# Half of the gate chunk's late adaptive units moved from TensorE to VectorE

## The reference, cut to what matters

```python
mod_l = jnp.split((silu(c) @ w_ada + b_ada)[:, None, :], 6, axis=-1)   # 2048 x 12288
mod_c = jnp.split((silu(c_ctx) @ w_ada + b_ada)[None, None, :], 6, axis=-1)
n_lat = modulate(rmsnorm(x, g_norm1), mod_l[0], mod_l[1])
n_ctx = modulate(rmsnorm(ctx, g_norm1), mod_c[0], mod_c[1])
...
z_lat = n_lat @ w_in ; z_ctx = n_ctx @ w_in[:, :o_g]     # columns U (S5), V (recurrence), gates
ya = s5_mixer(U) ; yb = lru_mixer(V) * gelu(z_lat[..., o_g:o_ga])
m = sigmoid(z_lat[..., o_ga:o_gb]) * (ya @ w_proj_a) + sigmoid(z_lat[..., o_gb:]) * (yb @ w_proj_b)
h_lat = x + mod_l[2] * (m @ w_out)
f_lat = modulate(rmsnorm(h_lat, g_norm2), mod_l[3], mod_l[4])
h_lat = h_lat + mod_l[5] * peer_ffn(f_lat, ...)
```

## Time and profile before

| | |
|---|---|
| time, median of 3 runs | 2298.59 us (2296.38 to 2298.80) |
| profiled execution: its time, its span | 2300.83 us, 2299.0 us |
| mean granted TensorE clock in it | 0.985 of full speed |
| busy: PE, DVE, ACT, POOL | 2000.0, 1369.5, 472.4, 1056.5 us |
| HBM read, written | 772.12 MB, 9.47 MB |

### The profile page before, as it was taken

How to read it: one execution, slowest core, us unless ns; L and a number is a source line. 1 busy time by engine, 2 the same in 40 slices (tenths; PEclk the granted TensorE clock), 3 DMA queues, 4 the chain that set the end, 5 groups by cost and what they waited for, 6 DMA issues and landing times.

```text
span 2299.0 us, 21921 instructions
## 1 busy us (share of the span) xinstructions
PE 2000.0 (87%) x8122; PEld 1158.5 (50%) x8122; DVE 1369.5 (60%) x2153; ACT 472.4 (21%) x1019; POOL 1056.5 (46%) x929
## 2 busy tenths in 40 slices
PE   6999999999999999979997998978877777777776
PEld 3443348888888878755553544423322222222222
DVE  5645964788873434774565455556556665655644
ACT  3116740344431000111101110111111011111011
POOL 0012323898991100164554445655555555555542
PEclk9999999999999999989999999999999999999999
DMA  9977885445558998899999999999999999999996
GB/s 338 336 226 201 313 302 173 135 144 147 147 150 301 355 325 297 314 392 415 422 421 413 421 420 419 422 421 421 422 421 422 421 421 421 421 422 422 421 422 271
DMA packets 249598, 787.26 MB, mean 342 GB/s; under 512 B 25578, under 2 KB 162994, under 8 KB 174354
## 3 DMA queue, kind: packets, MB, share of 16 engines
q0 software_dynamic: 83792, 574.96, 61.4%
q1 hardware_dynamic: 154020, 201.45, 26.4%
q10 hardware_dynamic: 11680, 9.44, 1.3%
HBM read 772.12 MB, written 9.47 MB: 340 GB/s over the span
## 4 chain that ended last, share of the span: by engine, by line
PE 45%; DMA 36%; POOL 13%; issue 4%; DVE 2%; ACT 1%; ACTq 0%; DVEq 0%; POOLq 0%
DMA vb<-in_peer_v,eidx 33%; PE ps L2396 14%; PE ps L1355 8%; PE ps L2255 5%; PE ps L2317 4%; PE ps L1562 4%; PE ps L1325 3%; PE ps L1340 2%; POOL vb L1767 1%; PE ps L1591 1%; PE ps L1300 1%; POOL nT L1767 1%; POOL big L609 1%; POOL big L578 1%; POOL big L581 1%
## 5 line engine op out<-in xcount | busy, mean ns | idle before, releaser
L2396 PE MATMUL ps<-vb,diag 128*128 128x512 f32 x2048 | 943.9, 609 | 229.8 <-DMA vb<-in_peer_v,eidx 227.7
L2396 PEld LDWEIGHTS ps<-vb,diag 128*128 128x128 f32 x2048 | 378.2, 192 | 782.5 <-issue 403.7
L1767 POOL DMA_INDIRECT vb<-in_peer_v,eidx x256 | 403.2, 1575 | 516.8 <-PE ps L2396 498.3
L2176 DVE CUSTOM_DVE_ANT_0 nT<-nT,f 128x2048 f32<-128x2048 f32 x167 | 381.9, 2291 | 315.0 <-DMA nT<-in_peer_u,eidx 314.6
L1355 PE MATMUL ps<-nT,w_ring 128*128 128x256 f32 (+1 forms) x1472 | 381.6, 417 | 0.0
L1355 PEld LDWEIGHTS ps<-nT,w_ring 128*128 128x128 f32 x1472 | 276.2, 190 | 95.6 <-issue 65.9
L2176 DVE CUSTOM_DVE_ANT_0 mT<-mT,f 128x2048 f32<-128x2048 f32 x84 | 192.2, 2292 | 158.3 <-DMA mT<-in_peer_u,eidx 158.0
L1767 POOL DMA_INDIRECT nT<-in_peer_u,eidx x167 | 190.6, 1141 | 68.4 <-issue 49.7
L1940 ACT ACTIVATE gel<-hd 128x2 f32<-128x2 f32 (+1 forms) x130 | 26.2, 202 | 905.8 <-DVE hd L2176 905.7
L2317 PE MATMUL ps<-fT,w_ring 128*128 128x256 f32 x448 | 101.2, 385 | 8.5 <-issue 7.8
L1767 POOL DMA_INDIRECT mT<-in_peer_u,eidx x84 | 93.4, 1112 | 32.1 <-issue 25.0
(11 more groups left out here) (416 smaller groups left out, 2176.5 us busy)
## 6 DMA issues: line engine op xcount, KB each, us to landing
w_ring<-in_w_ada SPq DMA_DIRECT2D x80, 1024.0 KB, 8.4
w_ring<-in_w_in SPq DMA_DIRECT2D x50, 1024.0 KB, 8.1
w_ring<-in_w_ada POOLq DMA_DIRECT2D x16, 1024.0 KB, 5.7
w_ring<-in_peer_w_query SPq DMA_DIRECT2D x16, 1024.0 KB, 17.6
w_ring<-in_w_proj_b SPq DMA_DIRECT2D x8, 1024.0 KB, 7.1
w_ring<-in_w_proj_a SPq DMA_DIRECT2D x8, 1024.0 KB, 7.4
w_ring<-in_w_out SPq DMA_DIRECT2D x8, 1024.0 KB, 6.3
vb<-in_w_out SPq DMA_DIRECT2D x5, 1024.0 KB, 12.8
```

What stands on the lines that cost most here:

```text
L1767: pool.indirect_dma_start(row, None, table, bass.IndirectOffsetOnAxis(ap=eidx[:, i % 3, j:j + 1], axis=0))\
L2176: v.tensor_tensor_reduce(u_buffer(m), u_buffer(m), f[:, i // HEADS], 1.0, 0.0, ALU.mult, ALU.add, hd[:, i % 2, m % K:m % K + 1]).then_inc( ...
L2396: last = pe.matmul(ps[:, 4 * tile + c, :], diag[:, m % NDIAG], vb[m % NV][:, c * 512:(c + 1) * 512], start=(r == 0), stop=(r == HEADS * K ...
```

## The change

Units 0 to 7 of chunk 2 become rows. There are now 24 rows: 0 to 7 of chunk 2, 8 to 23 of chunk 3, all through slot 4. Rows 0 to 3 are used ahead of the recurrence (`EARLY_ROWS`), 4 to 18 in it, two in each step and one in the last, 19 to 23 behind the multiplies of gate columns 0, 1, 4, 5 and 6 (`GATE_ROWS`). TensorE keeps units 8 to 15 of chunk 2, one in each column from U column 8 on. The sum of rows 0 to 7 has its own place (`first_sums`, two pieces of 1024 columns, one of them the memory of `kzero`), and `last_rows(0)` adds it into bank 6 behind gate column 5. `late_rows(0)` moves from the end of the recurrence to the place behind gate column 6. GpSimd loads rows 1 to 4 ahead of the first U store, rows 21 to 23 behind the loads of L562, and only then does `store_mods(0)`. Slot 4 returns to the ring when row 23 is used, and the gate columns' halves stay in slots 0 to 2.

```diff
-LATE_PER_PAIR = {3: (1, 0), 4: (3, 1), 5: (3, 1), 6: (3, 1), 7: (2, 1)}
+LATE_PER_PAIR = {3: (1, 0), 4: (1, 1), 5: (1, 1), 6: (1, 1), 7: (1, 0)}
+ON_VECTOR, EARLY_ROWS, GATE_ROWS = 8, 4, (0, 1, 4, 5, 6)
...
-        late = [(c, k) for c in LATE_CHUNKS for k in range(KD)]
+        late = [(LATE_CHUNKS[0], k) for k in range(ON_VECTOR, KD)]
+        rows = [(LATE_CHUNKS[0], k) for k in range(ON_VECTOR)] + [(c, k) for c in LATE_CHUNKS[1:] for k in range(KD)]
+        n_rows = ON_VECTOR + KD
...
-        freed_by[4] = (last_used, KD)
+        freed_by[4] = (last_used, n_rows)
...
-        last_wide = n + 1
-        n_slot = [turn[(2 * last_wide + 2) % 3]]
+        first_stage = len(pairs) - NSTAGE
+        for n in range(n + 2, first_stage):
+            plan_first(n, turn[2 * n % 3])
+            plan_second(n, turn[(2 * n + 1) % 3])
+        n_slot = [turn[2 * first_stage % 3]]
...
-        for n in range(last_wide + 1, len(pairs)):
+        for n in range(first_stage, len(pairs)):
             plan_first(n, next_slot())
             plan_second(n, next_slot())
...
-        kzero = sb("kzero", [H, G, H])
+        kz_all = sb("kzero", [P, G * H])
+        kzero = kz_all[0:H].rearrange("p (g h) -> p g h", g=G)
+        first_b = sb("first_b", [P, D - G * H])
         Cc = sb("Cc", [P, 2, G, H])
...
+        first_sums = [(kz_all, 0, G * H), (first_b, G * H, D)]
...
+        rows_of = [0, ON_VECTOR] + [ON_VECTOR + q * KD for q in range(1, NLATE)]
...
                     pool.wait_ge(last_used, k)
-                at = LATE_CHUNKS[1] * D
+                c, k = rows[k]
+                at = c * D
                 pool.dma_start(row_view(w_ring[:, 4]), t["w_ada"][0, k * P:(k + 1) * P, at:at + D])\
...
+            for n in range(1, EARLY_ROWS + 1):
+                load_row(n)
             for k in range(KW):
-                if 2 * k + 2 < KD:
-                    load_row(2 * k + 2)
+                load_row(EARLY_ROWS + 2 * k + 1)
                 pool.wait_ge(acc_free, U0 + k + 1)
                 for b in range(8):
                     at = (b % GS) * NC
                     dst = u_dram[:, :, 2 * k + b // GS, at:at + NC].rearrange("s h c -> h s c")
                     pool.dma_start(dst, zu[b * H:(b + 1) * H, k % 2]).then_inc(u_out, 16)
-                if 2 * k + 3 < KD:
-                    load_row(2 * k + 3)
...
+            for n in range(EARLY_ROWS + 2 * KW + 1, rows_of[2]):
+                load_row(n)
             store_mods(0)
             pool.wait_ge(mods_out, 32)
             load_bias(1)
...
-            row_vector(0)
+            for n in range(EARLY_ROWS):
+                row_vector(n)
             for k in range(KW):
                 q_of(k)
-                row_vector(2 * k + 1)
+                row_vector(EARLY_ROWS + 2 * k)
                 scans(k)
                 if k < KW - 1:
-                    row_vector(2 * k + 2)
...
 
                 v.wait_ge(mods_out, 32 * q + 16)
-                if q == 0:
-                    v.wait_ge(ada_used, KD * (NFIRST + 1))
-                else:
-                    v.wait_ge(last_sum, q)
+                v.wait_ge(last_sum, q + 1)
                 tt(mod_rows[:], ps[:, (6, 7, 0)[q], :], mod_rows[:], ALU.add).then_inc(mod_free, 1)
 
...
+                if k in GATE_ROWS:
+                    row_vector(EARLY_ROWS + 2 * KW - 1 + GATE_ROWS.index(k))
                 if k in (2, 3):
                     input_weights(k - 2)
+                if k == KW - 2:
+                    late_rows(0)
 
             lag_zero()
...
-                k = ada_n[0] % KD
+                n = ada_n[0] - NFIRST * KD
+                k = ON_VECTOR + n
                 w = row_view(unit(pe, ada_at[ada_n[0]]))
                 ada_n[0] += 1
                 for j in range(4):
                     last = pe.matmul(ps[32 * j:32 * j + 32, bank, :], scol[:, k, :], w[:, j * 512:(j + 1) * 512],
-                                     start=(k == 0), stop=(k == KD - 1))
+                                     start=(n == 0), stop=False)
...
-                pe.wait_ge(last_used, KD * q)
+                pe.wait_ge(last_used, rows_of[q + 1])
                 if q == 2:
...
-                    for total, lo, hi in (sums if q == 1 else [(fin_sum, 0, D)]):
+                    for total, lo, hi in (first_sums, sums, [(fin_sum, 0, D)])[q]:
...
-                    columns_by_halves(V0 + 2 * c, 0, 2 * T, [(n, j) for n in range(2) for j in range(2)])
+                    columns_by_halves(V0 + 2 * c, 0, 2 * T, [(0, 0), (1, 1)])
                     break
-                spots = ((), ()) if c < KW // 2 else ((7, 15), (7, 15))
+                spots = ((), ()) if c < KW // 2 else ((7,), (7,))
...
             for c in range(1, KW // 2):
                 for _ in columns(G0 + 2 * c, T, 2 * T):
                     pass
+                if c == KW // 2 - 2:
+                    last_rows(0)
             lag_zero()
             last_rows(1)
```

More of the change, by code:

```diff
@@ L241, in build @@
                 plan_last()
-        assert n_late[0] + len(last_at) == len(late)
+        assert n_late[0] == len(late) and len(last_at) == len(rows)
         def load_unit(eng, u):
@@ L557, in _ @@
                     pool.dma_start(dst, zu[b * H:(b + 1) * H, k % 2]).then_inc(u_out, 16)
[L558 to L559 removed]
+                load_row(EARLY_ROWS + 2 * k + 2)
             pool.wait_ge(u_out, 128 * KW)
@@ L1103, in scans, with row_vector @@
                 v.wait_ge(lru_done, k + 1)
-            def row_vector(k):
-                v.wait_ge(row_in, 16 * (k + 1))
+            def row_vector(n):
+                v.wait_ge(row_in, 16 * (n + 1))
                 w = row_view(w_ring[:, 4])
-                for n, (total, lo, hi) in enumerate(sums):
+                k = rows[n][1]
+                for x, (total, lo, hi) in enumerate(first_sums if n < ON_VECTOR else sums):
                     if k == 0:
@@ L1227, in fin_vector @@
             def fin_vector(k):
-                last_unit(v, unit, last_at[KD + k], fin_sum, scol, k, (last_used, KD + k + 1))
+                n = rows_of[2] + k
+                last_unit(v, unit, last_at[n], fin_sum, scol, k, (last_used, n + 1))
             v.wait_ge(y_full, NSTAGE)
```

26 lines of the change are left out of this document (13 added, 13 removed).

## The result

The change makes the kernel slower: 2341.11 us (median of 6 runs, 2337.42 to 2344.64) against 2298.7 us (6 runs, 2296.38 to 2305.59), a ratio of 1.0188, 95% interval 1.0177 to 1.02. The forecast was 2313 us, range 2303 to 2328: the direction came as forecast, and so did the order of the steps, but the shift is about three times as large and one cause of it, TensorE's clock, was in no term. The profiled execution took 2341.57 us, its span is 2339.8 us, mean granted clock 0.979.

A forecast was written before the change was run, and what follows sets the result against it. TensorE bounded the columns and gate columns, GpSimd the S5 stages. Row trips, ring waits and GpSimd's tail put its second build +13.6 us: span 2312.6, median 2312.2, with half the possible collision 2313 us; range 2303 to 2328.

The forecast's parts named there:

- What bounds the kernel, and what is taken away: TensorE bounds columns and gate columns, GpSimd the S5 stages; eight units leaving the columns save 8.0 us, last_rows(0) returns 1.0.
- Step 1: Ahead of the recurrence: rows 1 to 3 a round trip apart, so the recurrence starts at 219.5, 30.9 us later.
- Step 2: In the recurrence: rows 4 to 18 cost 15 round trips of 8.6 us; scans end at 354.6, +7.6 us.
- Rival (a): Row transfers take longer, 6.5 us to land: scans end at 368, +27 us, 2326 us; chance 0.15 (beyond +20).
- Step 3: At TensorE's second gate column, which waits behind row 17: all 8.0 us saved are waited away, and 7.0 us more.
- Step 4: Ring in the gate columns, three slots not five: third and fourth pair each wait 2.8 us, +5.7; TensorE leaves at 404.0.
- Step 5: Tail on GpSimd: rows 21 to 23, store and bias load precede stage 0's preparation; second build +14.0, less slack +13.6 us.
- possible collision: GpSimd's and VectorE's work colliding in the stage 0 preparation: a microsecond or two more possible.
- From the mark on: After the start of GpSimd's second build (407.50 us before), stages, projections and experts follow; nothing gives the delay back.
- (b): Rows and w_in land at the floor, 5.0 us: +7.5 us, 2306 us; chance 0.12 together with (d).
- (d): The gate columns' ring costs nothing, halves land within 3.5 us: +8, 2306 us; chance 0.12 together with (b).
- (c): Not slower: early rows land while VectorE idles, TensorE stays the bound and keeps the 8.0 us: 2296 us; chance 0.06.

## Why the prediction was wrong

The mark was forecast at 421.5 and came at 446.57. The 25 us between go step by step. The sums below lay one trace beside the forecast; they say where the time was lost in it, not what the end would be without one of the terms.

**What bounds the kernel, and what is taken away: right.** With one row ahead of the recurrence, or with short rows, TensorE gets all of its 8.0 us and enters the gate columns at 327.7 to 327.9.

**Step 1: right.** 219.5 forecast, 220.98 measured; +1.5.

**Step 2: mis-sized, the first large error.** The term was 15 x 8.6 us = 129, and from row 3 (218.34) to row 18 (355.62) are 137.3, which is 9.15 a row. The scans end at 364.36, not 354.6: +9.8, of which 1.5 is step 1's. The median landing was right (5.7 taken, 5.5 measured), but the median was the wrong figure to multiply. From one row to the next it takes the longer of two times, gap by gap: the trip of the row, or VectorE's own work up to it (8.6 to 8.8 us with scans or a convolution in between, 5.1 with neither). Seven of the 15 gaps are VectorE's own, and there a short trip gives nothing back. In the other eight VectorE waits, 22.2 us in all. Four gaps with long trips (rows 4, 10, 11, 13, at 10.7 to 11.5 us; row 4 was 8.6 in flight) are together 9.8 above 8.6 each, and all the shorter gaps give back 1.5. Rival (a), with 6.5 us for every landing, came nearest (scans at 368, 2326 us), though the median landing was no longer than I took.

**Step 3: right in form.** The second gate column follows row 17: 354.43, forecast 346.3, +8.1. Row 17 itself was done at 350.2, forecast 339.9, +10.3; 2.2 of that came back, mostly because ScalarE loads no table ahead of the last roots. The trace before has them without a table load too (328.14), and I had taken the 1.28 us from the first group's row.

**Step 4: the wrong pair, and a missing term.** TensorE leaves the gate columns at 419.75, forecast 404.0: +15.75. Of it 8.1 comes from step 3. The gaps ahead of the second, third and fourth pair were forecast as 0, 2.8 and 2.8 and are 1.02, 5.52 and 1.85 (0.85 idle behind 1.0 of `last_rows(0)`, which is hidden in the wait as forecast: the half goes out at 400.5 and the pair starts 5.3 later, the same 5.3 as without `last_rows(0)` in the run with the tail taken off GpSimd). That is +2.8 in sum: 3.7 more ahead of gate column 4, on which the tail hangs, and 0.9 less ahead of the last pair. **The clock was not in the sum at all: 12.46 - 10.5 and 16.43 - 14.05, +4.4.** The remaining 0.4 is rounding and where the two traces begin. The Trainium skill, "TensorE: Matmul & The Clock Gate", section "The HAM clock gate", has the idle array at 1.2 GHz and the busy one at 2.4. The trace of the change agrees (0.50 from 352 to 356 us, behind the wait of 7.43). The rows of the kernel before could not show it, since they have no wait there; the prediction that made such waits should have asked what the engine does behind one.

**Step 5: three terms too small.** Gate column 4's multiply was forecast at 380.9 and came at 397.54: +16.6, made up of step 3 (8.1), the waits (3.7), the clock (4.4) and 0.4 of rounding. The two trips of rows 22 and 23 took 18.9 us, not 17.2: +1.7. The store's landing was taken from a quiet place, 2.4 us; beside weight loads it took 6.5 from issue to the next instruction. The trace before had the same store in this very stretch, at 9.7 us from issue to issue, and I passed over it:

```profile
348.04 0.66 POOL L546 DMA_DIRECT2D mods_dram<-mod_rows  x1 [0.51 <-DVE mod_rows L1163]
357.78 0.59 POOL L520 DMA_DIRECT2D mod_rows<-in_b_ada  x1 [9.08 <-DMA mods_dram<-mod_rows]
```

From the end of `late_rows(0)` (420.71) to the preparation are 7.4 us, not 3.3: +4.1. The preparation takes 18.5 us, not 15.7, +2.8: single steps on both engines are longer where VectorE's two-input steps now run beside GpSimd's, as in the prediction's own remark on a possible collision; no run here takes this cause away alone. 16.6 + 1.7 + 4.1 + 2.8 = 25.2, the 25.1 but for rounding.

**From the mark on: right.** Nothing gives it back: +39.1 at the mark, +40.8 in the span.

**The rivals.** (b) and (d) fell: short landings do bring the 8.0 us back, but they were had only at an eighth of the bytes. The ring is not free: three slots alone cost 5.2 at the mark. (c) fell in its sign: with rows 1 to 3 early, halves and the tail mended too, TensorE's 8.0 us did not reach the end.

## What to carry to other kernels

Work moved to an engine with idle time must be priced by what feeds it. One buffer whose next load waits for the last use makes a chain of trips. Such a chain is not the median trip times the count: take, gap by gap, the longer of the trip and the engine's own work, with trips as different as a trace shows them. Where the two are about equal, as in most gaps here, a long trip adds and a short one hardly pays back (9.8 us against 1.5).

A forecast that puts a wait of several microseconds in front of TensorE owes a term for its clock. One that moves a small store or a shared stage to another time owes a new duration, read from the same stretch of the trace and not from a quiet one.

Check what hangs on each moved step: here a wait of 2.8 us came out as 5.5, and since the last rows hung on the column behind it, it delayed GpSimd's tail by as much.

## What the runs showed of the hardware

- Landing and bytes: 128 KB land in 2.3/2.4/7.8 us (least, median, most), 1 MB in 4.9/5.5/12.4 on the same queue. Estimated from the least of each: 0.92 MB more in 2.6 us, 353 GB/s, beside some 2 us that do not depend on bytes. The Trainium skill, "DMA: Bandwidth & Descriptors", section "Anatomy of one DMA", has 2.0 us and 436 GB/s: an estimated 2.3 us for the small one, which the trace bears out, and 4.4 for the large, which no load reached.
- Halves of 512 KB took 5.1 us in the median, almost as long as 1 MB: in the company of other loads the length of a transfer says little about when it lands.
- TensorE's durations grew behind all the longer waits looked at (3.40, 3.78, 3.88, 4.15, 4.65, 4.68, 5.52, 5.90, 7.43), and behind some of 2 to 3 us (2.16, 2.44 and 2.83, but not 2.17, 2.73 or 2.76). Where they grew, the windows show a granted clock of 0.50 to 0.73 in the first microseconds behind the restart, and 1.00 where they did not.
- VectorE's two-input steps of 512 elements take 0.69 us alone and 1.4 to 1.6 beside GpSimd's of the same length, and GpSimd's 1.05 become 1.38; the preparation in which they meet took 2.8 us more.
